# Row numbers of the first expert tile from a comparison with the ranks of expert 0, and one summed set for the routing table and the gates

## The chip, the core and the metric

One Trainium2 chip, of which the kernel uses one core. The metric is device time in microseconds (us) of one execution, start to end. The kernel before takes 900.72 us (median of 3 runs, 900.62 to 901.5).

## What is computed

One step of a one-layer decoder trunk over 1056 tokens (a prompt of 1024 and 8 samples of 4), each a row of 1024 float32 numbers:

```python
x <- LN1(alpha * x + Mixer(x))      # one input projection, conv / pool / gated conv, one output projection
x <- LN2(alpha * x + HierMoE(x))

def hier_moe(xt):                                    # xt: 1056 x 1024
    g_logits = xt @ w_rg + b_rg                      # 4 expert groups, top 1
    e_logits = xt @ w_re + b_re                      # 4 experts in the chosen group, top 2
    top_w = softmax(top_v) * g_p
    for e in range(16):                              # SwiGLU, 1024 -> 512 -> 1024
        h = silu(xt @ w_gate[e]) * (xt @ w_up[e])
        y = y + gate[:, e:e + 1] * (h @ w_down[e])
```

## The kernel before, in words

The program is written engine by engine, with semaphores between the engines; each engine works through its own list in order. There are three parts: the mixer, the routing, and the expert tiles. A short last part adds up and normalises.

**Expert tiles.** Tokens are sorted by expert into tiles of 128 rows, each tile of one expert (here 26 tiles for 16 experts). Per tile, POOL fetches the rows from DRAM (`x1_rows`) by an indirect DMA (L670), PE turns them (8 transposes, L1293), ACT rounds them into a high part (L938 for the first tile) and DVE makes the low part (L1229); with high and low parts of rows and weights PE multiplies three times for each product (L1564 gate and up, in two halves of 24 matmuls each; L1580 down). The weights of an expert come in six units of 1 MB: units 0 to 3 hold gate and up, units 4 and 5 hold down. ACT makes each unit's high part, DVE the low part (`lo_unit`, L328). A tile's first half (`h == 0`) takes six matmuls from unit 0, six from unit 1 and so on, and waits for each unit's low part. After 18 matmuls of the second half PE turns the first half of the hidden values, which DVE has multiplied (L1243). SP reloads a unit for the next expert when its low part is made.

**Routing.** When all logits are there, DVE chooses for each token a group and two experts (L1134 to L1156: `Mb` is 1 where a token chose an expert). PE sums over the choices (L1510 to L1517): the rank of a token within each expert, and how many tokens each expert has. From the counts DVE makes the first and the last tile of each expert (L1161 to L1167), from ranks and first tiles each choice's place: its tile `tcol` and its row in the tile `rlf` (L1172 to L1183). Then come one-hot sets: `ohe`, which tile (L1187, 630 elements a partition), `oht`, the same times the token number and times a correction (L1189, L1191), and `ohp`, which row (L1194, two of 1152 elements). PE multiplies `ohp` by `oht` (L1524): the sum in PSUM is the table of row numbers for every tile. Meanwhile DVE makes the gates of the choices (L1199 to L1204), then takes the table out of PSUM (L1206, L1207). Only then POOL copies the first tile's column into `idxc` (L665), does a one-element add behind which the copy is sure to be written (L669), and sends the indirect DMA of the first rows (L670). While they travel, DVE splits the gates into three bfloat16 parts (L1211 to L1214), multiplies them into `ohe` (`otw`, three ops, L1216), PE sums these too (L1546, 105 columns), and DVE makes the low parts of units 1 and 2 (L328). After the first tile's rows are split, DVE adds up the gate parts (L1233 to L1235) and makes the low parts of units 3, 4 and 5.

POOL asks for the second tile's rows after the first rows have landed and PE has turned them: copy L665, add L669, DMA L670.

## Time and profile before

| | |
|---|---|
| median of 3 runs | 900.72 us |
| the profiled execution | 900.35 us |
| its span (first to last instruction) | 898.7 us |
| PE busy, DVE busy, ACT busy, POOL busy | 91%, 65%, 49%, 30% of the span |
| mean granted TensorE clock | 0.956 of full speed |
| logits complete, start of routing on DVE | 362.1 us |
| first indirect DMA sent | 381.4 us |
| PE starts the first expert tile | 389.4 us |

The profile lists instructions with start, duration and what released them, all in us from the start of the span. PE is the matmul engine, DVE the vector engine, ACT the scalar engine, POOL the general one, SP issues DMAs. A line such as L328 is a line of the kernel; a line in a helper stands for all its callers. The clock of PE is granted at one of two levels, 1.2 and 2.4 GHz, shown as 0.5 and 1.0.

### The profile page before, as it was taken

The numbers are of one execution on the slowest core, as the hardware profiler recorded it, in microseconds if no ns is written. First come the engines' busy times: TensorE is split into PE (matmuls) and PEld (weight loads), VectorE is DVE, ScalarE is ACT, GpSimd is POOL, SyncE is SP. The second block draws the span as 40 slices with busy tenths as digits, with TensorE's granted clock in tenths as the row PEclk, the third lists the DMA queues.
The fourth block names the chain that finished last, engine by engine and source line by source line (L and its number), as shares of the span: only waits on it lengthen the run. The fifth ranks groups of instructions, "written<-read, shape, count | busy, mean of one in ns | idle before, by whom it ended". The sixth has DMA issues, their size and how long they took to land.

```text
span 898.7 us, 12722 instructions
## 1 busy us (share of the span) xinstructions
PE 822.1 (91%) x4275; PEld 715.2 (80%) x4276; DVE 587.9 (65%) x732; ACT 442.2 (49%) x494; POOL 268.8 (30%) x259
## 2 busy tenths in 40 slices
PE   6999999999999999289999999999999999999900
PEld 6999999998788886168888888888888888888800
DVE  4099999957666555889889982158821614837148
ACT  5311132546633224338888883359733725846233
POOL 1423564562000000024433441224321313323225
PEclk9999999999999999579999999999999999999955
DMA  8211111103656331479999998149952663973164
GB/s 289 55 48 47 47 47 47 47 1 114 241 196 251 117 121 47 153 245 320 392 384 379 394 393 289 28 132 375 374 190 59 213 174 93 363 263 88 24 237 172
DMA packets 59407, 167.34 MB, mean 186 GB/s; under 512 B 6757, under 2 KB 25190, under 8 KB 55286
## 3 DMA queue, kind: packets, MB, share of 16 engines
q1 hardware_dynamic: 51318, 144.57, 43.0%
q0 software_dynamic: 8064, 22.45, 11.6%
q8 instruction: 14, 0.23, 0.1%
q14 instruction: 11, 0.09, 0.0%
HBM read 144.79 MB, written 28.24 MB: 193 GB/s over the span
## 4 chain that ended last, share of the span: by engine, by line
PE 89%; DVE 6%; DMA 2%; ACT 1%; issue 1%; POOL 0%; SPq 0%; POOLq 0%; ACTq 0%; DVEq 0%
PE PS L1564 32%; PE PS L1315 19%; PE PS L1580 16%; PE PS L1494 10%; PE PS L1293 6%; DVE C L1073 1%; PE PS L1342 1%; PE PS L1465 1%; PE PS L1382 1%; DVE RAW L1270 1%; PE PS L1446 1%; DVE BIG L387 1%; DMA sum_rows<-F,MIX 1%; DMA F<-in_x_prompt 1%; DMA F<-x_rows,MIX 0%
## 5 line engine op out<-in xcount | busy, mean ns | idle before, releaser
L1564 PE MATMUL PS<-BIG,TH 128*128 128x512 f32 x1248 | 296.3, 394 | 1.5 <-DVE TH L1229 1.5
L1564 PEld LDWEIGHTS PS<-BIG,TH 128*128 128x128 f32 x1248 | 233.9, 189 | 49.5 <-issue 1.9
L1315 PE MATMUL PS<-BIG,WD 128*128 128x352 f32 x1080 | 177.3, 325 | 0.0
L1315 PEld LDWEIGHTS PS<-BIG,WD 128*128 128x128 f32 x1080 | 174.9, 188 | 0.9
L328 DVE TENSOR_TENSOR BIG<-RAW,BIG 128x2048 fp32r<-128x2048 f32 x64 | 145.1, 2288 | 24.3 <-ACT BIG L901 24.3
L1580 PE MATMUL PS<-WD,TH 128*128 128x512 f32 x624 | 155.8, 399 | 0.0
L1580 PEld LDWEIGHTS PS<-WD,TH 128*128 128x128 f32 x624 | 113.5, 189 | 21.9
L901 ACT ACTIVATE BIG<-RAW 128x2048 fp32r<-128x2048 f32 x64 | 119.2, 1908 | 15.5 <-PE PS L1494 7.9
L292 DVE SCALAR_TENSOR_TENSOR PS<-RAW,C,PS 128x512 f32<-128x512 f32 x174 | 115.4, 752 | 0.0
L1494 PE MATMUL PS<-BIG,WD 128*128 128x512 f32 (+1 forms) x432 | 100.7, 392 | 1.8 <-DVE BIG L387 1.8
L1494 PEld LDWEIGHTS PS<-BIG,WD 128*128 128x128 f32 (+1 forms) x432 | 76.7, 179 | 22.7 <-issue 1.3
L669 POOL TENSOR_TENSOR MIX<-C 128x1 f32<-128x1 f32 x28 | 33.5, 1198 | 189.2 <-PE PS L1293 189.0
L1243 DVE TENSOR_TENSOR F<-F,PS 128x256 f32<-128x256 f32 x52 | 21.8, 420 | 93.4 <-ACT F L944 81.1
L328 DVE TENSOR_TENSOR WD<-MIX,WD 128x2048 fp32r<-128x2048 f32 x32 | 72.0, 2289 | 9.6 <-ACT WD L901 9.6
L1293 PEld LDWEIGHTS PS<-C,F 128*128 128x128 f32 (+1 forms) x408 | 60.9, 188 | 13.9 <-issue 6.3
L1293 PE MATMUL PS<-C,F 128*128 128x128 f32 (+1 forms) x408 | 62.8, 284 | 7.5 <-DMA F<-in_x_prompt 6.7
L550 POOL TENSOR_TENSOR WD<-F,WD 128x1024 fp32r<-128x1024 f32 x17 | 41.0, 2409 | 76.5 <-ACT WD L718 76.3
L901 ACT ACTIVATE WD<-MIX 128x2048 fp32r<-128x2048 f32 x32 | 59.6, 1907 | 3.3 <-DMA MIX<-in_w_down 3.3
L1247 DVE TENSOR_TENSOR TH<-PS,TH 128x256 fp32r<-128x256 f32 x52 | 21.9, 421 | 56.4 <-ACT TH L950 33.4
L965 ACT ACTIVATE F<-PS,MIX 128x1024 f32<-128x1024 f32 x26 | 29.1, 1119 | 49.4 <-PE PS L1580 49.4
L692 POOL TENSOR_TENSOR MIX<-C 128x1 f32<-128x1 f32 x26 | 18.9, 728 | 108.1 <-ACT F L965 108.1
L693 POOL DMA_INDIRECT sum_rows<-F,MIX x26 | 41.9, 1610 | 7.8 <-issue 7.8
(203 smaller groups left out, 762.6 us busy)
## 6 DMA issues: line engine op xcount, KB each, us to landing
RAW<-in_w_gate SPq DMA_DIRECT2D x64, 512.0 KB, 7.1
RAW<-in_w_up SPq DMA_DIRECT2D x64, 512.0 KB, 9.3
MIX<-in_w_down SPq DMA_DIRECT2D x32, 1024.0 KB, 10.4
F<-in_w_in SPq DMA_DIRECT2D x17, 512.0 KB, 4.1
F<-in_x_prompt SPq DMA_DIRECT2D x10, 512.0 KB, 4.7
x_rows<-F SPq DMA_DIRECT2D x9, 512.0 KB, 2.6
sum_rows<-F SPq DMA_DIRECT2D x9, 512.0 KB, 3.6
RAW<-in_w_out SPq DMA_DIRECT2D x4, 1024.0 KB, 6.2
```

Of the source, the lines that this page charges most:

```text
L292: ins = eng.scalar_tensor_tensor(accs[h] if j < TAPS - 1 else outs[h], ins_[h], w, accs[h], ALU.mult, ALU.add)
L328: eng.tensor_tensor(by_row(u, l), raw_rows(u), by_row(u, unit_parts(u)[0].bitcast(F32)), ALU.subtract).then_inc(S("unit_lo"), 1)
L550: pool.tensor_tensor(win[:, q, 1], wraw[q].rearrange("p (k m) -> p k m", k=KD), win[:, q, 0].bitcast(F32), ALU.subtract).then_inc(S("win_l ...
L669: pool.tensor_tensor(carrier[:, 0:1], epsc, epsc, ALU.add)
L693: pool.indirect_dma_start(acc_dram, bass.IndirectOffsetOnAxis(ap=scat, axis=0), yrow, None, compute_op=ALU.add).then_inc(S("y_stored"), 16)
L901: act.activation(by_row(u, h), raw_rows(u), ACT.Copy).then_inc(S("unit_hi"), 1)
L965: act.activation(yrow, PS[:, 5:7, :].rearrange("p b n -> p (b n)"), ACT.Copy, scale=gates[:, ds(t, 1)]).then_inc(S("y_copied"), 1)
L1293: return pe.transpose(out, in_, ident[0:n, 0:n])
L1315: mm = pe.matmul(bank(3 * q + g, GRP), win[:, q, ws, c, :], xT[:, xs_, c, g * GRP:(g + 1) * GRP], start=(c == 0 and ws + xs_ == 0), stop=( ...
L1494: mm = pe.matmul(bank(out_bank(i, h), rows=M), mhl[:, i % 2, ms, c, 0:M], wo[:, ws, c, h * 512:(h + 1) * 512], start=(c == 0 and ms + ws = ...
L1564: mm = pe.matmul(bank(h), xe[:, xs_, c, :], w, start=(c == 0 and xs_ + ws == 0), stop=(c == KD - 1 and xs_ == 1))
L1580: mm = pe.matmul(bank(5 + h), he[:, hs, c, :], wd[:, ws, c, h * 512:(h + 1) * 512], start=(c == 0 and hs + ws == 0), stop=(c == KF - 1 and ...
```

## The change

For the first tile alone the row numbers are made without the table. A token that chose expert 0 sits in the first tile in the row of its rank within expert 0, so one comparison of `igf` (row numbers less 1024) with `key0` (rank less 1024 where the token chose expert 0) gives the one-hot set `ohf` (1152 elements a partition, bfloat16). PE multiplies it by `vc0`, two columns: the token numbers and a correction (9 matmuls, into bank 5); DVE adds these to `idxc` directly, and POOL sends the first indirect DMA from that, with no copy and no add of its own.

The table is made afterwards, and together with the gates: `otw` now has five sets of columns (token number, correction, three gate parts) and PE sums 175 columns in one set of 18 matmuls, which stands behind the 8 transposes of the first rows. DVE makes the first two of the five; the three products with the gate parts move from DVE to POOL. The gates' values are made ahead of the ranks. The low parts of units 1 and 2 move from before the split of the first rows to behind the table.

```diff
@@ gpsimd
+                gather_rows()
+
+            def gather_rows():
                 pool.indirect_dma_start(xg, None, x1_dram, bass.IndirectOffsetOnAxis(ap=idxc, axis=0),
...
+            pool.wait_ge(S("x1_stored"), 16 * NT)
+            pool.wait_ge(S("first_index"), 1)
+            gather_rows()
+            pool.wait_ge(S("columns_hot"), 1)
+            for h in range(3):
+                pool.tensor_tensor(otw[:, :, :, 2 + h, :], ohe,
+                                   part[h].rearrange("p k (i m) -> p k i m", m=1).to_broadcast((P, 2, NT, NTAB)),
+                                   ALU.mult).then_inc(S("gate_hot"), 1)
+            pool.wait_ge(S("rows_in"), 16)
             pool.wait_ge(S("table_ready"), 1)
-            index(0)
-            pool.wait_ge(S("x1_stored"), 16 * NT)
-            gather(0)
-            pool.wait_ge(S("rows_in"), 16)
             index(1)
             pool.wait_ge(S("xe_turned"), 1)
             gather(1)
@@ vector
+            dve.tensor_copy(vc0[:, :, 0], tokid[:, 0:NT]).then_inc(S("first_values"), 1)
...
+            dve.wait_ge(S("exps"), 2)
+            do(dve.tensor_reduce(gsum, ge, AX, ALU.add))
...
+            do(dve.tensor_tensor(wgt[:, 1], wgt[:, 0], ex, ALU.mult))
             dve.wait_ge(S("ranked"), 1)
+            do(dve.scalar_tensor_tensor(key0, Mb[:, :, 0], -float(FAR), rk[:, :, 0], ALU.mult, ALU.add))
+            dve.tensor_scalar(vc0[:, :, 1], key0, -1.0, pm, ALU.mult, ALU.add).then_inc(S("first_values"), 1)
+            dve.wait_ge(S("x1_ready"), NT)
+            dve.tensor_tensor(ohf, igf.rearrange("p (i m) -> p i m", i=1).to_broadcast((P, NT, P)),
+                              key0.rearrange("p (i m) -> p i m", m=1).to_broadcast((P, NT, P)), ALU.is_equal
+                              ).then_inc(S("first_hot"), 1)
             counts_ps = bank(7)[:, NT * NE:(NT + 1) * NE]
...
+            dve.wait_ge(S("first_sum"), 1)
+            do(dve.tensor_copy(firstf, bank(5, 2)))
+            dve.scalar_tensor_tensor(idxc, firstf[:, 0:1], padc, firstf[:, 1:2], ALU.add, ALU.add
+                                     ).then_inc(S("first_index"), 1)
+            do(dve.tensor_copy(part[0], wgt))
...
-            do(dve.tensor_tensor(ohe, it.rearrange("p (k i m) -> p k i m", k=1, i=1).to_broadcast(four),
-                                 tcol.rearrange("p k (i m) -> p k i m", m=1).to_broadcast(four), ALU.is_equal))
-            do(dve.tensor_tensor(oht[:, :, :, 0, :], ohe, tokid[:, 0:NT].rearrange("p (k i m) -> p k i m", k=1, m=1
+            dve.tensor_tensor(ohe, it.rearrange("p (k i m) -> p k i m", k=1, i=1).to_broadcast(four),
+                              tcol.rearrange("p k (i m) -> p k i m", m=1).to_broadcast(four), ALU.is_equal
+                              ).then_inc(S("columns_hot"), 1)
+            dve.wait_ge(S("columns_hot"), 1)
+            do(dve.tensor_tensor(otw[:, :, :, 0, :], ohe, tokid[:, 0:NT].rearrange("p (k i m) -> p k i m", k=1, m=1
...
-            for h in range(3):
-                dve.tensor_tensor(otw[:, :, :, h, :], ohe,
...
-            lo_unit(dve, 0, 1)
-            lo_unit(dve, 0, 2)
...
             ins.then_inc(S("xe_lo"), 1)
-            dve.wait_ge(S("gate_sum"), 1)
-            do(dve.tensor_copy(gatep, bank(7, 3 * NTAB)))
...
+            dve.wait_ge(S("table_sum"), 1)
+            do(dve.tensor_copy(tabf, bank(6, 5 * NTAB)))
+            dve.scalar_tensor_tensor(table, tabf[:, 0:NTAB], padc, tabf[:, NTAB:2 * NTAB], ALU.add, ALU.add
+                                     ).then_inc(S("table_ready"), 1)
+            for u in (1, 2, 3):
+                lo_unit(dve, 0, u)
...
-            for u in (3, 4, 5):
+            for u in (4, 5):
                 lo_unit(dve, 0, u)
@@ tensor
+            pe.wait_ge(S("first_values"), 2)
+            pe.wait_ge(S("first_hot"), 1)
+            for i in range(NT):
+                M = rows_of(i)
+                mm = pe.matmul(bank(5, 2), ohf[0:M, i], vc0[0:M, i], start=(i == 0), stop=(i == NT - 1))
+            mm.then_inc(S("first_sum"), 1)
...
             mm.then_inc(S("xe_turned"), 1)
+            pe.wait_ge(S("gate_hot"), 3)
+            for c in range(2):
+                pe.wait_ge(S("one_hot"), c + 1)
+                for i in range(NT):
+                    M = rows_of(i)
+                    mm = pe.matmul(bank(6, 5 * NTAB), ohp[0:M, c, i], otw[0:M, c, i].rearrange("p h m -> p (h m)"),
+                                   start=(c + i == 0), stop=(c == 1 and i == NT - 1))
+            mm.then_inc(S("table_sum"), 1)
```

How the lists of the engines change, at two places. First DVE, from the one-hot sets to the last unit of expert 0. Before:

```order
L1187 TENSOR_TENSOR RAW<-MIX 128x630 [waits x1_ready,route_steps]
L1189 TENSOR_TENSOR RAW<-RAW,MIX 128x18x35 [waits route_steps]
L1191 TENSOR_TENSOR RAW<-RAW,MIX 128x18x35 [waits route_steps]
L1194 TENSOR_TENSOR RAW<-MIX 128x1152 [waits route_steps]
...
L1216 TENSOR_TENSOR MIX<-RAW,MIX 128x18x35 [waits route_steps]
L1216 TENSOR_TENSOR MIX<-RAW,MIX 128x18x35 x2
L328 TENSOR_TENSOR BIG<-RAW,BIG 128x2048 [waits unit_hi] x2
L1229 TENSOR_TENSOR TH<-PS,TH 128x512 [waits half_hi]
L1229 TENSOR_TENSOR TH<-PS,TH 128x512 [waits xe_hi]
L1233 COPY MIX<-PS 128x105 [waits gate_sum]
```

and now (L331 is the old L328, L1241 the old L1229):

```order
L1221 TENSOR_TENSOR RAW<-MIX 128x630 [waits route_steps]
L1225 TENSOR_TENSOR MIX<-RAW,MIX 128x18x35 [waits columns_hot]
L1227 TENSOR_TENSOR MIX<-RAW,MIX 128x18x35 [waits route_steps]
L1230 TENSOR_TENSOR RAW<-MIX 128x1152 [waits route_steps]
L1230 TENSOR_TENSOR RAW<-MIX 128x1152
L1241 TENSOR_TENSOR TH<-PS,TH 128x512 [waits half_hi]
L1241 TENSOR_TENSOR TH<-PS,TH 128x512 [waits xe_hi]
L1245 COPY MIX<-PS 128x175 [waits table_sum]
L1246 SCALAR_TENSOR_TENSOR MIX<-MIX 128x35 [waits route_steps]
L331 TENSOR_TENSOR BIG<-RAW,BIG 128x2048 [waits unit_hi] x3
```

The three products of 18x35 are gone from DVE, and the two units that stood ahead of the split of the rows stand behind the table. Second POOL, around the first two fetches. Before:

```order
L665 COPY MIX<-MIX 128x1 [waits table_ready]
L669 TENSOR_TENSOR MIX<-C 128x1 [waits index_copied,x1_stored]
L670 DMA F<-x_rows,MIX 128x1024
L665 COPY MIX<-MIX 128x1 [waits rows_in]
L669 TENSOR_TENSOR MIX<-C 128x1 [waits index_copied,xe_turned]
L670 DMA F<-x_rows,MIX 128x1024
```

and now:

```order
L676 DMA F<-x_rows,MIX 128x1024 [waits first_index,x1_stored]
L685 TENSOR_TENSOR MIX<-RAW,MIX 128x18x35 [waits columns_hot]
L685 TENSOR_TENSOR MIX<-RAW,MIX 128x18x35 x2
L668 COPY MIX<-MIX 128x1 [waits table_ready,rows_in]
L672 TENSOR_TENSOR MIX<-C 128x1 [waits index_copied,xe_turned]
L676 DMA F<-x_rows,MIX 128x1024
```

The first DMA stands ahead of the table's work and the three products stand between it and the second fetch, which now waits for the table.

## Rows read from the trace of the kernel before

**Rows 1.** The page, part 4: the chain that ended last, shares by engine.
```profile
PE 89%; DVE 6%; DMA 2%; ACT 1%; issue 1%; POOL 0%; SPq 0%; POOLq 0%; ACTq 0%; DVEq 0%
```

**Rows 2.** Busy time by stretch: us, each engine busy (instructions), PEclk, DMA share, GB/s.
```profile
380.00:390.00 10.00, 4.70 (x28) 3.63 (x29) 9.56 (x16) 1.49 (x3) 4.72 (x6) 0.50 0.37 117
390.00:400.00 10.00, 10.00 (x38) 8.09 (x37) 6.90 (x4) 2.80 (x3) 1.62 (x1) 0.82 0.97 326
```

**Rows 3.** The chain that ended last, in order of time: start us, us, what.
```profile
381.41 4.45 DMA F<-x_rows,MIX
...
385.91 1.99 PE PS L1293 x8
...
389.38 11.80 PE PS L1564 x42
...
409.43 9.53 PE PS L1564 x42
```

**Rows 4.** Timeline of DVE, routing to first tile: start us, us, line, op, [idle before].
```profile
369.22 0.17 DVE L1161 TENSOR_SCALAR MIX<-PS 128x16 int32<-128x16 f32 x1 [1.12 <-PE PS L1517]
...
370.44 0.30 DVE L1172 SCALAR_TENSOR_TENSOR MIX<-MIX,PS 128x144 f32<-128x144 f32 x1
...
373.25 0.82 DVE L1187 TENSOR_TENSOR RAW<-MIX 128x630 f32<-128x630 f32 x1 [0.20 <-DVE MIX L1183]
...
375.80 2.63 DVE L1194 TENSOR_TENSOR RAW<-MIX 128x1152 bf16<-128x1152 f32 x2
...
379.47 0.17 DVE L1204 TENSOR_TENSOR MIX<-MIX 128x9 f32<-128x9 f32 x1
...
379.94 0.26 DVE L1207 SCALAR_TENSOR_TENSOR MIX<-MIX 128x35 uint32<-128x35 f32 x1
...
380.74 0.18 DVE L1214 TENSOR_TENSOR MIX<-MIX 128x18 bf16<-128x18 f32 x1
380.96 2.26 DVE L1216 TENSOR_TENSOR MIX<-RAW,MIX 128x630 bf16<-128x630 f32 x3
383.14 4.49 DVE L328 TENSOR_TENSOR BIG<-RAW,BIG 128x2048 fp32r<-128x2048 f32 x2
387.69 0.69 DVE L1229 TENSOR_TENSOR TH<-PS,TH 128x512 fp32r<-128x512 f32 x1
...
389.15 0.26 DVE L1233 COPY MIX<-PS 128x105 f32<-128x105 f32 x1
...
397.54 0.42 DVE L1243 TENSOR_TENSOR F<-F,PS 128x256 f32<-128x256 f32 x1 [1.06 <-ACT F L944]
```

**Rows 5.** Timeline of PE: the sums of the gates.
```profile
383.28 2.11 PE L1546 MATMUL PS<-MIX,RAW 128*128 128x105 bf16 x18 [3.98 <-DVE MIX L1216]
```

**Rows 6.** Timeline of POOL: around the second tile's fetch.
```profile
385.92 1.75 POOL L665 COPY MIX<-MIX 128x1 uint32<-128x1 uint32 x1 [3.16 <-DMA F<-x_rows,MIX]
...
388.68 1.06 POOL L670 DMA_INDIRECT F<-x_rows,MIX  x1 [0.52 <-issue]
394.90 1.62 POOL L665 COPY MIX<-MIX 128x1 uint32<-128x1 uint32 x1 [5.17 <-DMA F<-x_rows,MIX]
```

**Rows 7.** Timeline of POOL and DVE in the mixer, 46 to 50 us.
```profile
46.42 2.39 POOL L550 TENSOR_TENSOR WD<-F,WD 128x1024 fp32r<-128x1024 f32 x1
46.48 2.68 DVE L277 TENSOR_TENSOR MIX<-RAW,C 128x248 f32<-128x248 f32 x1 [18.36 <-POOL RAW L560]
49.08 0.90 DVE L277 TENSOR_TENSOR MIX<-RAW,C 128x248 f32<-128x248 f32 x2
```

**Rows 8.** POOL's groups by shape: count, busy us, mean ns, idle before.
```profile
L590 POOL TENSOR_TENSOR MIX<-RAW 128x1038 f32<-128x1038 f32 x2 | 3.8, 1914 | 0.0
L591 POOL TENSOR_TENSOR RAW<-RAW 128x144 f32<-128x144 f32 x2 | 0.8, 422 | 0.0
```

**Rows 9.** DMA issues, 380 to 560 us: median us from issue to landing.
```profile
F<-x_rows,MIX POOLq DMA_INDIRECT x11, 7.0
```

**Rows 10.** Waits, 380 to 860 us: who for whom, us in total, times, longest.
```profile
ACT WD L901 <- DMA MIX<-in_w_down: 0.8, 1, 0.8
```

More of the change, by code:

```diff
@@ L207, in build @@
         wrem = [mx(2 * NT).rearrange("p (k i) -> p k i", k=2) for _ in range(2)]
+        part = [wpart[0][:, 0], wpart[0][:, 1], wpart[1][:, 0]]
         ohp = RAW[:, OFF_BC:OFF_BC + NT * P].bitcast(BF16).rearrange("p (k i m) -> p k i m", k=2, i=NT)
-        oht = RAW[:, OFF_BC + NT * P:OFF_BC + NT * (P + 2 * NTAB)].bitcast(BF16
-                  ).rearrange("p (k i h m) -> p k i h m", k=2, i=NT, h=2)
-        ohe = RAW[:, OFF_BC + NT * (P + 2 * NTAB):OFF_BC + NT * (P + 4 * NTAB)
-                  ].rearrange("p (k i m) -> p k i m", k=2, i=NT)
-        tabf = mx(2 * NTAB)
+        ohe = RAW[:, OFF_BC + NT * P:OFF_BC + NT * (P + 2 * NTAB)].rearrange("p (k i m) -> p k i m", k=2, i=NT)
+        ohf = (RAW[:, OFF_BC + NT * (P + 2 * NTAB):OFF_BC + NT * (P + 2 * NTAB) + NT * P // 2].bitcast(BF16)
+               .rearrange("p (i m) -> p i m", i=NT))
+        igf, key0, pm = mx(P), mx(NT), mx(1)
+        vc0 = mx(NT).bitcast(BF16).rearrange("p (i w) -> p i w", w=2)
+        firstf = mx(2)
+        tabf = mx(5 * NTAB)
         table = mx(NTAB).bitcast(U32)
         idxc = mx(1).bitcast(U32)
-        otw = mx(3 * NT * NTAB).bitcast(BF16).rearrange("p (k i h m) -> p k i h m", k=2, i=NT, h=3)
-        gatep = mx(3 * NTAB)
+        otw = mx(5 * NT * NTAB).bitcast(BF16).rearrange("p (k i h m) -> p k i h m", k=2, i=NT, h=5)
         gates = mx(NTAB)
@@ L1519, in _ @@
             mm.then_inc(S("ranked"), 1)
-            for c in range(2):
-                pe.wait_ge(S("one_hot"), c + 1)
-                for i in range(NT):
-                    M = rows_of(i)
-                    mm = pe.matmul(bank(6, 2 * NTAB), ohp[0:M, c, i], oht[0:M, c, i].rearrange("p h m -> p (h m)"),
-                                   start=(c + i == 0), stop=(c == 1 and i == NT - 1))
-            mm.then_inc(S("table_sum"), 1)
+            pe.wait_ge(S("first_values"), 2)
[4 more added lines that the diff above has]
+            mm.then_inc(S("first_sum"), 1)
             def turn_xe(t):
@@ L1538, in turn_hid @@
                 mm.then_inc(S("hid_turned"), 1)
-            for c in range(2):
-                for i in range(NT):
-                    M = rows_of(i)
-                    if c + i == 0:
-                        pe.wait_ge(S("gate_hot"), 3)
-                    mm = pe.matmul(bank(7, 3 * NTAB), ohp[0:M, c, i], otw[0:M, c, i].rearrange("p h m -> p (h m)"),
-                                   start=(c + i == 0), stop=(c == 1 and i == NT - 1))
-            mm.then_inc(S("gate_sum"), 1)
             pe.wait_ge(S("rows_in"), 16)
```

41 lines of the change are left out of this document (15 added, 26 removed).

## The prediction, made before the changed kernel ran

> **What bounds the kernel now.** I read the page's chain first: PE holds 89% of it, DVE 6%, DMA 2% [rows 1]. PE cannot be helped by this change except where it waits, so I then read the busy time by stretch: from 380 to 390 us PE is busy 4.70 of 10 us and DVE 9.56 [rows 2]. That is the routing. The chain in order of time says what PE waits for there: the indirect DMA of the first rows, sent at 381.41 and landed 4.45 us later, 8 transposes, the split, and the first tile at 389.38 [rows 3]. After that the chain is PE alone to the last tile, so a first tile that ends earlier by x should end the kernel earlier by x, unless something else is late. The last view, DVE's timeline, tells what else: DVE has hardly a pause from the choices to unit 5. While the rows travel it makes three products (2.26 us) and the low parts of units 1 and 2 (4.49), and its split of the rows starts 0.06 us after those [rows 4]. The rows' travel is thus already full of DVE work; an earlier landing finds DVE in arrears. So the question is how far DVE's own list is shortened, and whether POOL's help is free.
>
> **How POOL and DVE get on.** POOL's 2.39 us operation of 46.42 ends at 48.81; a DVE product of two SBUF inputs that starts at 46.48 takes 2.68 us, to 49.16, while the next two take 0.90 together [rows 7]. It stood still until POOL had ended. The other way round, POOL's one-element copies at 385.92 and 394.90 take 1.75 and 1.62 us, and the first ends at 387.67, when the second of DVE's L328 has ended (383.14 + 4.49 = 387.63) [rows 4, 6]. I read this as: a DVE instruction with two SBUF inputs and a POOL instruction exclude each other for their whole length, and the waiting one goes at the next boundary. [...]
>
> **The sum, on the clock of the profile.** Each step by its rows.
> - Up to the choices: one added copy of 9 elements, 0.1 us. The choices are made at 368.10 (DVE idles 1.12 before 369.22) [rows 4].
> - The gates' six small operations move here: from the end of L1194 at 378.43 to the end of L1204 at 379.64 they took 1.2 us [rows 4]. The 1.12 us wait for the ranks covers them but for 0.1 to 0.2. At 369.5 `key0` and the correction follow, two at 0.2, then `ohf`, 1152 elements like each half of L1194 (2.63 / 2 = 1.31) [rows 4]: 371.2.
> - PE's 9 matmuls of two columns take at most half of the gates' 18 (2.11 / 2 = 1.05) [rows 5], and lie beside the counts, which took 369.22 to 370.44 = 1.22 [rows 4]: 372.4. Two small operations give `idxc`, 0.4 to 0.5 (L1207 is 0.26) [rows 4]: 372.9.
> - POOL sends the DMA at 373 to 374.1 (before, 1.21 us lay between L1207's end at 380.20 and the DMA at 381.41, copy and add included); with 4.45 us [rows 3] the rows land at 377.5 to 378.6, 7 to 8 us earlier than before. The transposes, 1.99 [rows 3], end by 380.6. None of that is on the path, as follows.
> - DVE goes on: four splits of the gates, 0.72 (380.20 to 380.92), then ranks to places, 370.44 to 373.25 = 2.81, `ohe` 0.82 [rows 4]: 377.2. Before, `ohe` ended at 374.07; this is the 3.1 us that the short cut costs.
> - From 377.2 DVE has two products and two one-hot sets, which took 374.10 to 378.43 = 4.33 [rows 4], and POOL its three products of 630 elements. POOL's price is not in the trace for this shape. From below: the step from 144 to 1038 elements is 1.49 us [rows 8], so 0.42 + 486 x 1.67 ns = 1.23. From nearby above: 2.39 x 630 / 1024 = 1.47 [rows 7]. I take 1.45, since L550 like these writes another type than it reads. A bfloat16 input on POOL is not shown; the outer end is the 2.39 of the full 1024. All of it excludes DVE's: 4.33 + 3 x 1.45 = 8.7, DVE free at 385.9, whichever begins; POOL done at about 384.6.
> - The Trainium skill, GPSIMD Engine Reference, When to use GPSIMD, says to keep two-input elementwise work on VectorE, GpSimd being about twice as slow; by that the three would cost 4.5 instead of 2.26 us, and the sum would be later by 0.2 than mine.
> - PE: 18 matmuls of 175 columns, by columns 2.11 x 175 / 105 = 3.5 [rows 5]; nine from 384.6, nine once the last one-hot set is there at 385.9: 387.9. Meanwhile DVE splits the rows, two at 0.69 [rows 4], to 387.3.
> - First tile: PE starts at about 388.0 instead of 389.38. DVE takes 175 columns (105 took 0.26; 0.35) and makes the table (0.26) [rows 4]: 388.5, then units 1, 2, 3 at 4.49 / 2 = 2.25 each: 390.8, 393.0, 395.3.  Six matmuls cost 6 x 9.53 / 42 = 1.36 at the full clock and up to twice that, 2.7, at the low one (the first tile's 42 took 11.80; the granted clock is 0.50 from 380 to 390, 0.82 from 390 to 400) [rows 2, 3]. So PE now waits for units 1, 2 and 3, and its first half ends at 395.3 + 1.36 = 396.7; before, 18 matmuls (4.1) ahead of 389.38 + 11.80 = 401.18, that was 397.1.
> - Gain 0.4 us. Next late is DVE: gates 0.4, units 4 and 5 4.49, first hidden product 0.42: 400.6, needed at 396.7 + 4.1 = 400.8 (before it was there at 397.96, three us ahead) [rows 4]. If this cover of 0.2 us goes, each further delay of DVE costs the same on PE.
>
> The later loads of expert 1 (units 1 to 5 are loaded when their low parts are made, now 3 to 5 us later) I cost at nothing: from 380 to 860 us ACT waited for weights once, 0.8 us [rows 10]. The three DVE products and POOL's copy and add for the first tile are removed at no gain of their own; they are in the sum.
>
> **Forecast:** 0.4 us less. The profiled execution of 900.35 becomes 899.95; the median of the runs is 0.37 above it, so 900.3. A measurement of this kernel tells 0.2%, 1.8 us, from no change. The bounds of POOL's price move DVE's list by 3 x (1.23 - 1.45) = -0.7 to 3 x (2.39 - 1.45) = +2.8.
>
> **Rivals.**
> 1. *POOL and DVE run side by side.* Then DVE and POOL are both done at 381.6, PE's table at 385.2, DVE's table at 385.8, unit 3 at 392.6, the first half at 393.9: 3.2 us less, with the hidden product (397.9) just in time. An earlier PE meets the weights where ACT already waited 0.8 us [rows 10], which may take up to as much back. 897.5 to 898.3. For it: the rows show full exclusion at two shapes only, neither with a bfloat16 result. [...] Against: [rows 6, 7]. Chance 0.16.
> 2. *The second fetch comes late (slower).* It now needs the table and then three turns of POOL against DVE's units: copy at 390.8, add at 393.0, DMA at about 393.6, which if shut out until 395.3 lands 7.0 us later [rows 9] at 402.3. PE wants these rows when its second half ends, 396.7 + 24 x 0.227 = 402.2. Before, they landed at 394.9 (389.74 + 5.17) [rows 6], six us ahead. It decides from 402.2 on: one turn missed (2.25 us, and once shut out behind unit 4, 2.2 more than in the sum) makes 404.5 to 404.7, PE waits 2.4, net +2.0 to +2.5: 902.7 to 903.2. Against: both copies in rows 6 got in at the first boundary they met. Chance 0.11.
> 3. *The clock stays low while PE waits for units.* Then six matmuls take up to 2.7 us, more than DVE's 2.25 a unit, the first half ends by 390.8 + 8.1 = 398.9, up to 1.8 later than before: up to 902.5. Against: the clock rose between 390 and 400 (0.82, so at about 393.6) behind PE work that began at 389.38 [rows 2, 3]; now PE works from 384.6. Chance 0.06.
> 4. *POOL's products are dear* (bfloat16 input, 2.39 each): +2.8 - 0.4 = +2.4, 903.1. Chance 0.07.
>
> The forecast has 0.60. Faster by over 1.8 us: rival 1, 0.16. Slower by over 1.8: rivals 2 and 4, 0.18. Within: 0.66. The range leaves out about 0.2: most of rival 1 and rival 4 with the far end of rival 2: 898.2 to 902.8; the forecast's own, with POOL between 1.23 and 1.6 and the second fetch up to 1 us late, is 899.6 to 901.7.
>
> **What would show it.** In the changed profile: the first indirect DMA at 373 to 374; POOL's three products (L685) and DVE's L1225 to L1230 stretched, each about as long as the other's turn, and ending at 385 to 386; PE's table at 388; L1579 with waits for L331; the first tile ending within 1 us of 409.4. Products of POOL of 1.5 us beside DVE's of normal length, or a first tile that ends before 408, would make it wrong; so would PE waiting for rows of the second tile at 402.

## The result, and the profile after the change

The changed kernel takes 902.66 us (median of 15 runs, 900.14 to 904.35), the kernel before 900.83 in the same comparison (15 runs): ratio 1.0016, 95% interval 1.0009 to 1.0023, or 1.4 us more (the two medians lie 1.8 apart). The forecast was 0.4 us less. The time lies in the range, and the change is below the 0.2% that the prediction took as the least to be told from no change; but it is clear of the noise here, and on the other side. Run twice more (below), the same kernel gave 0.9997 and 1.0004, neither clear of no change: its executions spread from 899.8 to 904.4, and in one of the three comparisons they fall in two separate groups, near 900.3 and near 903. What parts those that were profiled is shown below.

The profiled execution took 903.01 us, its span is 901.1. Where the time went is plainest from PE's start of each tile (the first L1579 of the tile in PE's timeline; L1564 before), in us; the last two columns are a repetition of the changed kernel and of its difference from before:

| tile | before | after | difference | after, repeated | difference |
|---|---|---|---|---|---|
| 0 | 389.38 | 386.56 | -2.82 | 386.88 | -2.50 |
| 1 | 409.27 | 407.14 | -2.13 | 407.58 | -1.69 |
| 7 | 516.09 | 513.84 | -2.25 | 514.38 | -1.71 |
| 8 | 533.91 | 535.58 | +1.67 | 533.93 | +0.02 |
| 25 | 836.23 | 838.03 | +1.80 | 836.37 | +0.14 |

The first tile gains much more than the 0.4 us forecast, and keeps it for seven tiles. Then one tile, that of expert 7, takes 21.74 us instead of 17.82, and from there on every tile is later than before. All other tiles from 1 on take 17.8 in both kernels. Behind the start of the last tile lie 63.0 us in the profile after, 62.5 before and 62.6 in the repeated one.

**At the front.** The timelines of DVE and POOL after the change (start us, us, line, op, idle before), to be read against [rows 4, 6]:

```profile
375.95 0.82 DVE L1221 TENSOR_TENSOR RAW<-MIX 128x630 f32<-128x630 f32 x1
376.80 0.82 DVE L1225 TENSOR_TENSOR MIX<-RAW,MIX 128x630 bf16<-128x630 f32 x1
377.65 1.74 DVE L1227 TENSOR_TENSOR MIX<-RAW,MIX 128x630 bf16<-128x630 f32 x1
379.43 4.59 DVE L1230 TENSOR_TENSOR RAW<-MIX 128x1152 bf16<-128x1152 f32 x2
383.94 1.27 DVE L1241 TENSOR_TENSOR TH<-PS,TH 128x512 fp32r<-128x512 f32 x2
386.04 0.34 DVE L1245 COPY MIX<-PS 128x175 f32<-128x175 f32 x1 [0.83 <-PE PS L1567]
386.42 0.26 DVE L1246 SCALAR_TENSOR_TENSOR MIX<-MIX 128x35 uint32<-128x35 f32 x1
386.59 6.69 DVE L331 TENSOR_TENSOR BIG<-RAW,BIG 128x2048 fp32r<-128x2048 f32 x3
```
```profile
373.48 1.12 POOL L676 DMA_INDIRECT F<-x_rows,MIX  x1 [10.58 <-DVE MIX L1198]
376.86 5.94 POOL L685 TENSOR_TENSOR MIX<-RAW,MIX 128x630 bf16<-128x630 f32 x3 [2.26 <-DVE RAW L1221]
386.83 2.09 POOL L668 COPY MIX<-MIX 128x1 uint32<-128x1 uint32 x1 [4.03 <-DVE MIX L1246]
389.06 2.06 POOL L672 TENSOR_TENSOR MIX<-C 128x1 f32<-128x1 f32 x1
391.30 2.94 POOL L676 DMA_INDIRECT F<-x_rows,MIX  x1 [0.17 <-issue]
400.36 0.40 POOL L668 COPY MIX<-MIX 128x1 uint32<-128x1 uint32 x1 [6.12 <-DMA F<-x_rows,MIX]
```

The two engines take turns. DVE's second product, alike in size to the first, takes 1.74 instead of 0.82, and the two one-hot sets 4.59 instead of 2.63 [rows 4], while POOL's three products take 5.94. PE in the same stretch, and the stretches as a whole (us, then each engine's busy time and instructions, the granted clock of PE, DMA share, GB/s; the DMA share is the mean busy share of the core's 16 DMA engines):

```profile
382.86 3.15 PE L1567 MATMUL PS<-MIX,RAW 128*128 128x175 bf16 x18 [3.12 <-POOL MIX L685]
386.56 4.31 PE L1579 MATMUL PS<-BIG,TH 128*128 128x512 f32 x12 [0.55 <-issue]
391.13 1.65 PE L1579 MATMUL PS<-BIG,TH 128*128 128x512 f32 x6 [0.26 <-DVE BIG L331]
393.33 5.74 PE L1579 MATMUL PS<-BIG,TH 128*128 128x512 f32 x24 [0.55 <-DVE BIG L331]
```
```profile
380.00:390.00 10.00, 6.59 (x27) 4.94 (x28) 9.14 (x8) 1.65 (x2) 5.83 (x4) 0.53 0.03 5
390.00:400.00 10.00, 9.19 (x40) 7.01 (x39) 9.90 (x8) 3.92 (x3) 4.07 (x2) 1.00 0.94 328
```

Against [rows 2], PE is busy 6.59 us of the ten from 380 on instead of 4.70, and its clock is at the upper level (1.00) through the next ten. But the DMA engines carry 5 GB/s from 380 to 390, where they carried 117. The loads of expert 1's weights wait for the low parts that DVE now makes behind the table. SP's timeline of the kernel before and then of the changed one, the loads of units 1, 2 and 4:

```profile
385.45 0.33 SPq L372 DMA_DIRECT2D RAW<-in_w_gate  x1
...
387.65 0.33 SPq L372 DMA_DIRECT2D RAW<-in_w_gate  x1
...
394.31 2.53 SPq L377 DMA_DIRECT2D MIX<-in_w_down  x2
```
```profile
388.90 0.33 SPq L375 DMA_DIRECT2D RAW<-in_w_gate  x1
...
391.11 0.33 SPq L375 DMA_DIRECT2D RAW<-in_w_gate  x1
...
395.84 2.53 SPq L380 DMA_DIRECT2D MIX<-in_w_down  x2
```

Units 1 and 2 start 3.45 us later, unit 3 1.2 and units 4 and 5 1.5 us later, while PE, which is going to use them, is 2 to 3 us earlier. From expert 2 on the loads go out 2.1 us earlier than before (unit 0 at 400.88 instead of 402.99), since they follow PE.

**At the tile of expert 7.** ACT's and PE's timelines after the change:

```profile
521.16 1.91 ACT L912 ACTIVATE BIG<-RAW 128x2048 fp32r<-128x2048 f32 x1
525.38 1.91 ACT L912 ACTIVATE BIG<-RAW 128x2048 fp32r<-128x2048 f32 x1 [2.31 <-DMA RAW<-in_w_up]
527.20 0.36 ACT L961 ACTIVATE TH<-PS 128x256 fp32r<-128x256 f32 x1
```
```profile
524.99 1.05 PE L1309 MATMUL PS<-C,F 128*128 128x128 f32 x8
528.15 1.93 PE L1595 MATMUL PS<-WD,TH 128*128 128x512 f32 x6 [2.11 <-DVE TH L1263]
...
530.16 5.58 PE L1595 MATMUL PS<-WD,TH 128*128 128x512 f32 x18
```

ACT stands 2.31 us before the high part of expert 8's unit 1, because half of that unit has not landed. Behind it in ACT's list stands L961, the high part of the hidden values (L950 before), then DVE's L1263, and PE waits for that, 2.11 us. The chain that ended last goes back through the same load ("511.04 14.26 DMA RAW<-in_w_up"): the load took 14.26 us from its issue. Behind its wait PE's matmuls are stretched, 18 of them to 5.58 us.

In the kernel before ACT made the high parts of units 0 and 1 in one go here:

```profile
523.17 3.94 ACT L901 ACTIVATE BIG<-RAW 128x2048 fp32r<-128x2048 f32 x2 [0.23 <-PE PS L1564]
```

The two take 1.91 each, so that of unit 1 began at about 525.2, behind a pause of 0.1 us. The same half unit landed at 525.12 there, and at 525.30 in the changed kernel: it came just in time before, and it comes no earlier now. The changed kernel asks for it 2.0 us earlier, at the end of unit 0's high part (523.07), and waits.

In the repeated profile of the changed kernel the rows of PE read:

```profile
528.08 1.65 PE L1595 MATMUL PS<-WD,TH 128*128 128x512 f32 x6 [1.49 <-DVE TH L1263]
...
529.72 4.38 PE L1595 MATMUL PS<-WD,TH 128*128 128x512 f32 x18
```

There the wait is 1.49, and 18 matmuls take 4.38. The granted clock tells the two apart: from 530 to 535 us it is 0.73 in the first profile and 1.00 in the second. So the loss is a load that comes later than ACT wants it, and in some executions a fall of PE's clock behind the wait on top of it. In the first comparison the mean granted clock of an execution fits that: 0.958 or 0.959 in the seven fastest (900.14 to 902.62 us), 0.954 to 0.957 in the eight slowest (902.66 to 904.35). In the two others the clocks of fast and slow executions overlap, and the seven without a fall are themselves 2.5 us apart, so the fall is not all that parts them. The tile takes 19.55 us in the repeated profile, 1.7 over the 17.82 before; in the first it is 3.9 over, 0.6 of the difference from a longer wait and 1.6 from the slower matmuls (1.93 - 1.65, 5.58 - 4.38, and two transposes between them).

Why is that load late? Busy time by stretch, the kernel before and then the changed one:

```profile
395.00:415.00 20.00, 20.00 (x96) 16.71 (x95) 15.44 (x12) 15.05 (x13) 8.68 (x7) 1.00 0.87 305
415.00:520.00 105.00, 105.00 (x498) 87.82 (x497) 94.39 (x66) 92.94 (x78) 43.35 (x35) 1.00 1.02 382
...
560.00:600.00 40.00, 40.00 (x194) 33.59 (x193) 9.24 (x14) 14.80 (x19) 7.28 (x13) 1.00 0.22 41
```
```profile
395.00:415.00 20.00, 20.00 (x95) 16.76 (x95) 19.03 (x14) 16.94 (x15) 5.84 (x7) 1.00 1.01 382
415.00:520.00 105.00, 105.00 (x499) 87.93 (x498) 94.44 (x67) 92.79 (x77) 43.41 (x36) 1.00 1.03 387
```

The first eight experts have one tile each, so each of their tiles brings six new units of weights. From 415 us on the DMA engines are busy all the time in both kernels (share 1.0, 382 to 387 GB/s), and the loads fall behind: the time from issue to landing grows over the stretch. For units 4 and 5 of expert 1, and of expert 8 (DMA issues of 388.5 to 399 us and of 519 to 523, KB each, median us to landing):

```profile
MIX<-in_w_down SPq DMA_DIRECT2D x2, 1024.0 KB, 8.0
```
```profile
MIX<-in_w_down SPq DMA_DIRECT2D x2, 1024.0 KB, 14.8
```

Expert 8 has four tiles, so that fewer loads are wanted, and from 560 to 600 us the share is 0.22. The tile of expert 7 is thus the last of the stretch, where the backlog is largest, and unit 1 is what ACT asks for early in a tile. In the kernel before the same tile had no such wait, PE being 2.2 us later.

### The profile page after: what moved, and what is told of

Read it like the earlier page. It is cut to its first block, busy times and chain, and to the rows that moved or that the text cites. A ratio compares the mean times of both kernels' runs of the same rounds, so it can differ in the third digit from the quotient of the medians.

```text
span 901.1 us, 12711 instructions
## 1 busy us (share of the span) xinstructions
PE 823.7 (91%) x4266; PEld 715.8 (79%) x4267; DVE 590.3 (66%) x734; ACT 441.6 (49%) x494; POOL 273.2 (30%) x262
## 4 chain that ended last, share of the span: by engine, by line
PE 87%; DVE 7%; DMA 3%; issue 1%; ACT 1%; POOL 1%; SPq 0%; ACTq 0%; POOLq 0%; DVEq 0%
PE PS L1579 30%; PE PS L1331 19%; PE PS L1595 15%; PE PS L1510 10%; PE PS L1309 6%; PE PS L1481 2%; DMA RAW<-in_w_up 2%; DVE C L1084 1%; PE PS L1358 1%; PE PS L1398 1%; DVE BIG L331 1%; DVE RAW L1286 1%; PE PS L1462 1%; DMA sum_rows<-F,MIX 1%; DVE BIG L390 1%
## 5 line engine op out<-in xcount | busy, mean ns | idle before, releaser
L1579 PE MATMUL PS<-BIG,TH 128*128 128x512 f32 x1248 | 296.2, 393 | 1.4 <-DVE BIG L331 0.8
L1579 PEld LDWEIGHTS PS<-BIG,TH 128*128 128x128 f32 x1248 | 233.3, 189 | 49.7 <-DVE BIG L331 1.8
L331 DVE TENSOR_TENSOR BIG<-RAW,BIG 128x2048 fp32r<-128x2048 f32 x64 | 145.0, 2289 | 21.9 <-ACT BIG L912 21.8
L331 DVE TENSOR_TENSOR WD<-MIX,WD 128x2048 fp32r<-128x2048 f32 x32 | 72.0, 2288 | 10.3 <-ACT WD L912 10.2
L1263 DVE TENSOR_TENSOR TH<-PS,TH 128x256 fp32r<-128x256 f32 x52 | 21.9, 422 | 59.5 <-ACT TH L961 36.2
```

Of the source, the lines that this page charges most:

```text
L331: eng.tensor_tensor(by_row(u, l), raw_rows(u), by_row(u, unit_parts(u)[0].bitcast(F32)), ALU.subtract).then_inc(S("unit_lo"), 1)
L1579: mm = pe.matmul(bank(h), xe[:, xs_, c, :], w, start=(c == 0 and xs_ + ws == 0), stop=(c == KD - 1 and xs_ == 1))
```

## The experiments

Theory (A): the DMA engines are the bound from 389 to 530 us; the lead of PE and the late start of the loads (A1) add up to what is lost in the tile of expert 7, and with less to carry, or an earlier start, the front's gain stays. By A2 the late start costs nothing. Rivals: the loss is one of ACT's order, of PE's clock, or of the one chip; or only PE's lead counts. Each comparison has its own runs of the kernel before beside it (medians 900.78 to 901.21).

**Less to load.** For experts 3 to 5 only the first half of unit 5 is loaded, 1.6 MB less in all.

```diff
-                sp.dma_start(unit_raw(u), src).then_inc(S(f"unit_raw{u}"), 16)
+                sp.dma_start(unit_raw(u)[:, 0:rows, :], src[:, 0:rows, :]).then_inc(S(f"unit_raw{u}"), 16)
...
+            with sp.Fori(3, 6) as e:
+                load_expert(e, 1)
```

In the changed kernel:

> The changed kernel, but unit 5 of experts 3, 4 and 5 is loaded by half (0.5 MB less each; the other half is stale, so these experts' down products are not the reference's). Theory A: the changed kernel's first tile ends 2.1 us earlier and PE keeps that for seven tiles; it loses it in the tile of expert 7, where ACT waits 2.3 us for weights of expert 8 because the loads have fallen behind. With 1.5 MB less ahead of it, some 4 us of loading at 390 GB/s, that wait is gone: no wait of ACT for a load near 525 us, the clock stays at 1.0 there, and the time is the one before less about 2.2: 898.6 us. Theory B: the loss there has another cause (code, order of the engines) and does not hang on the volume loaded: 902.7 us as the changed kernel.

In the kernel before:

> The kernel before with the same half loads of unit 5 of experts 3, 4 and 5. It is the control. Theory A: there the loads are just in time (ACT waits once, 0.8 us, and PE not at all), so less to load gives nothing: 900.8 us, within 0.3. If the cut itself sped up the program, this one would fall as well, to 899 or less, and after_cut would prove nothing.

Measured 898.83 us, ratio 0.9974 (0.9961 to 0.9986), and 900.29, ratio 0.9992 (0.9978 to 1.0005). In the first the tile of expert 7 takes 17.8, ACT waits for no load, and unit 1's landing takes 10.8 us instead of 14.3. The late load is the loss, and without it the change is worth 1.5 us against this control, 2 against the kernel before.

**Less to scatter.** Tiles are filled up to 128 rows; the rows behind an expert's last token were added into a row that nobody reads. Here they are left out.

```diff
-                                        compute_op=ALU.add).then_inc(S("y_stored"), 16)
+                                        bounds_check=TOK - 1, oob_is_err=False, compute_op=ALU.add).then_inc(S("y_stored"), 16)
```

In the changed kernel:

> The changed kernel, except that the scatter leaves out the rows behind an expert's last token (their row number is beyond the table), which otherwise are added to a row that nobody reads: 26 x 128 - 2112 = 1216 rows of 4 KB, some 5 MB of writes and as much reading for the addition. What is computed stays the same. Theory A (the DMA engines are busy all the time from 395 us on and fall behind the loads by some us until expert 8; less traffic brings the loads forward): the last part of unit 1 of expert 8 lands 2 us earlier or more, ACT's wait of 2.3 us in the tile of expert 7 goes, and the time is 898.6. Rival B (rows of the scatter cost the engines that carry the loads nothing, or the loads are bound by something else than the engines): the wait stays at 2 us and the time is that of the changed kernel, 900.9 to 902.7.

In the kernel before:

> The kernel before with the same scatter that leaves the rows behind an expert's last token out. Control: there PE stands 2.8 us later at tile 0, and ACT's wait for expert 8's unit 1 was 0.2 us, so theory A expects no change, 900.6 to 900.9. If less traffic is worth time for a reason of its own, this one is faster too, and what after_skip gains more than this one is what the wait had cost.

Measured 898.93 us, ratio 0.9969 (0.9957 to 0.9981), and 900.64, ratio 0.9992 (0.9978 to 1.0005). The rows of the late load, from the DMA issues of 510.5 to 513.5 us, in the changed kernel and then with the leaner scatter:

```profile
RAW<-in_w_up SPq DMA_DIRECT2D x1, 512.0 KB, 14.3
```
```profile
RAW<-in_w_up SPq DMA_DIRECT2D x1, 512.0 KB, 9.9
```

Against its control the change is worth 1.7 us here. Rows of POOL's scatter thus cost the engines that SP's loads use. The DMA share alone would not have told these kernels from the changed one: from 415 to 520 us it is 1.02 with the shorter loads (371 GB/s) and 0.99 with the leaner scatter (369 GB/s), and both keep PE's lead. The Trainium skill, DMA: Bandwidth & Descriptors, "Issuing engines are not separate DMA queues", says that DMAs of all engines run on the same 16 DMA engines and interleave; these two runs agree.

**The changed kernel again**, beside these and beside a later set.

> The changed kernel once more, nothing edited, as the measure for the three kernels beside it. Theory A (the 2.8 us that tile 0 gains are given back in the tile of expert 7, where ACT waits 2.3 us for the last part of expert 8's unit 1 and PE 2.1 us for ACT, with a clock that falls behind that wait in some executions and not in others): 900.9 to 902.7, the tile of expert 7 takes 20.2 us without a fall of the clock and 21.8 with one, against 17.8 in the tiles beside it. Rival B (the loss seen was one chip's, not the kernel's): 898.6, all tiles alike.

> The changed kernel once more, as the measure for the three beside it: 900.2 to 902.7, with executions in two groups, near 900.3 where the clock holds in the tile of expert 7 and near 903 where it falls behind PE's wait.

Measured 900.75 (0.9997, 0.9983 to 1.0011): eight executions from 899.81 to 901.07 and four from 902.49 to 903.69. Then 901.88 (1.0004, 0.9989 to 1.0018), 900.92 to 902.85; its profile shows the wait of 2.1 us with the 18 matmuls at 5.66.

**ACT's order.** The load that is late stands ahead of the hidden values in ACT's list; here it stands behind them.

```diff
-                    for u in (0, 1):
-                        act.wait_ge(S("unit_used"), 6 * t + u + 1)
-                        hi_unit(e + 1, u)
+                    act.wait_ge(S("unit_used"), 6 * t + 1)
+                    hi_unit(e + 1, 0)
...
+                if last:
+                    act.wait_ge(S("unit_used"), 6 * t + 2)
+                    hi_unit(e + 1, 1)
```

> The changed kernel, except that ACT makes the high part of the next expert's unit 1 behind the high part of the hidden layer's first half instead of ahead of it, in every expert's tile. Theory A (PE's 2.1 us in the tile of expert 7 are ACT's queue: the load that is late stands there ahead of the hidden values that PE wants, and PE doesn't want unit 1 itself before the next tile): PE no longer waits for the hidden values, the tile of expert 7 takes 17.8 us, and the lead of tile 0 stays, unless the late load is missed at the start of the next tile: 898.6 to 899.5. Rival B (PE is bound by the load itself, whatever the order of ACT): the same 2 us are lost at the start of the tile of expert 8, and the time is 900.9 or above.

Measured 907.6 us, ratio 1.0064 (1.0047 to 1.0081). ACT no longer waits for a load, but each such tile takes 18.4 us instead of 17.8: unit 1's low part comes later on DVE and stands ahead of the second half of the hidden values there. That wait of PE is about half of the 0.6 us. The row of PE's waits (us in total, times, longest) is from 386 to 860 us:

```profile
PE PS L1597 <- DVE TH L1265: 4.8, 15, 0.3
```

Both theories missed; the order that loses once in the tile of expert 7 saves 0.6 us in the tiles of other experts.

**PE kept busy while it would wait.** Sixteen matmuls of 256 columns more, in the tile of expert 7 (`"busy"` marks that expert's tile).

```diff
+                for _ in range(16 if last == "busy" else 0):
+                    pe.matmul(bank(7, 2 * P), TRI[:, 1, :], TRI[:, :, :].rearrange("p s m -> p (s m)"), start=True, stop=True)
...
-            expert_tiles(pe, tile)
+            expert_tiles(pe, tile, 7)
```

> The changed kernel, with 16 matmuls of 256 columns without use, into a free bank, in the tile of expert 7 alone, between the transposes of the next rows and the wait for the low part of the hidden values, where PE stood for 2.1 us. Theory A: the wait itself stays (the weights come when they come), but the clock, which fell to 0.5 from 529 to 533 us behind that wait, stays at 1.0, which gives back about 1.8 us: 900.9 us. If the fall of the clock costs nothing beside the wait: 902.7 us. If the matmuls only delay: up to 904.

Measured 901.53 (1.0001, 0.9988 to 1.0014), 900.25 to 902.38.

```profile
526.39 1.91 PE L1597 MATMUL PS<-TRI 128*128 128x256 bf16 x16
529.13 1.70 PE L1604 MATMUL PS<-WD,TH 128*128 128x512 f32 x6 [0.84 <-DVE TH L1270]
...
530.82 4.37 PE L1604 MATMUL PS<-WD,TH 128*128 128x512 f32 x18
```

1.91 us of work and 0.84 of wait: PE starts the next step at the same distance behind the load as before, and none of the 12 executions is above 902.38, where the upper group of the repeated comparison began at 902.49. The wait was time in which PE could do other work. That the clock never falls so is likely by these numbers, not shown beyond them, since a profile of the next experiment has the full wait and no fall either.

**The products back on DVE.** The three gate products of L685 are made by DVE.

```diff
-            pool.wait_ge(S("columns_hot"), 1)
-            for h in range(3):
-                pool.tensor_tensor(otw[:, :, :, 2 + h, :], ohe,
...
+            for h in range(3):
+                dve.tensor_tensor(otw[:, :, :, 2 + h, :], ohe,
```

> The changed kernel with the three products of the gate parts back on DVE, behind its own two and ahead of the one-hot sets; POOL does none. If POOL and DVE exclude each other (forecast): DVE is free at about 383.3 instead of 384.0, its products take 0.82 and 0.75, the one-hot sets 1.31 each again, the table's sum is ready about 1.0 us earlier (385 instead of 386) and the first tile ends about 1.0 earlier (406.1). The total then hangs on the loads (theory A): the gain is lost in the tile of expert 7, 902 to 903 us. If POOL's products had run beside DVE's for free: DVE's list is longer by 2.3 us and the first tile ends 2 us later, 409; the total is 901 to 905.

Measured 900.59 (0.9992, 0.9977 to 1.0006).

```profile
376.67 0.81 DVE L1216 TENSOR_TENSOR RAW<-MIX 128x630 f32<-128x630 f32 x1
377.51 0.82 DVE L1220 TENSOR_TENSOR MIX<-RAW,MIX 128x630 bf16<-128x630 f32 x1
378.37 0.82 DVE L1222 TENSOR_TENSOR MIX<-RAW,MIX 128x630 bf16<-128x630 f32 x1
379.22 2.26 DVE L1225 TENSOR_TENSOR MIX<-RAW,MIX 128x630 bf16<-128x630 f32 x3
381.40 2.62 DVE L1229 TENSOR_TENSOR RAW<-MIX 128x1152 bf16<-128x1152 f32 x2
```

With POOL still, every DVE operation has its own length again, and from the start of the mask `ohe` to the last one-hot set it is 7.35 us (376.67 to 384.02) instead of 8.06 (375.95 to 384.01). Handing three products to POOL cost 0.7 us net. The tile of expert 7 still loses time, PE's wait there being 2.1.

**PE late, or loads late.** The changed kernel starts PE earlier and the loads later. First the 16 added matmuls in the tile of expert 2, which takes the lead away (`expert_tiles(pe, tile, 2)` in the diff above):

> The changed kernel, except that PE makes 16 matmuls of 256 columns more in the tile of expert 2 (into a bank that nobody reads, 1.9 us), so that PE's lead over the kernel before falls from 2.2 us to 0.3 before the tile of expert 7. Theory A (the lead can't be kept past the late load of expert 8 in any case): the wait in the tile of expert 7 shrinks to 0.3 us or nothing, that tile takes 17.8 to 18.1 us, and the time is that of the changed kernel without the clock's fall, 900.5, with none of its executions above 902; the 1.9 us of work cost nothing. Rival B (the lead is worth its time to the end, and the loss in tile 7 is one of its own): 1.9 us on top of the changed kernel, 902.6 or above.

Measured 900.45 (0.9994, 0.9985 to 1.0002), eleven of the twelve executions between 899.82 and 901.75. By the time, 1.9 us of added work cost nothing, as theory A had it. The profile, which is of the slowest execution (903.09), does not bear it out: there PE waits 2.57 us in the tile of expert 7, its lead over the kernel before being 0.48. The load itself landed at 527.5 there, 2.2 us later than in the changed kernel, about as much as PE had been held up. So a small lead alone does not save an execution from the late load, and the landing is not fixed in time whatever PE does. A landing is told in 16 parts; 15 of this one were in at 523.87, and the last came 3.7 us behind them. Why is open.

Then the loads of expert 1 a step later, in both kernels, PE's own order unchanged:

```diff
-            load_expert(1)
+            for u in range(6):
+                wait_lo(sp, 0, min(u + 1, 5) if u else 0)
+                load_unit(sp, 1, u)
```

In the changed kernel:

> The changed kernel, except that SP issues the loads of expert 1's units 1 to 4 one step of expert 0's low parts later (each 2.2 us; unit 5 as it was). PE's work and its order are the same. Theory A1 (the DMA engines, without a break from 389 to 530 us, carry what the late start of expert 1's loads leaves behind through to the last load of the stretch): ACT's wait in the tile of expert 7 grows from 2.3 to 4.5 us, that tile takes 22 us or more, and the time is 902.9 to 904.5. Theory A2 (only PE's earlier start matters; a late start of the loads is made up on the way): the wait stays at 2.3 us, 900.5 to 902.5.

In the kernel before:

> The kernel before with the same loads of expert 1 a step later (units 1 to 4, by 2.2 to 4.4 us), so that they start as late as in the changed kernel while PE starts tile 0 as late as before. Theory A1 (start of the loads): ACT's wait in the tile of expert 7 is 2.4 us in place of 0.2, the tile takes 20 to 22 us, and the time is 903. Theory A2 (only PE's lead): no wait, 900.8.

Measured 903.53 (1.0023, 1.0009 to 1.0036) and 902.28 (1.0015, 1.0001 to 1.0030; before beside it 900.99). PE's timelines of the changed kernel in the tiles of experts 5 and 7, then of the kernel before in that of expert 7:

```profile
493.59 1.65 PE L1597 MATMUL PS<-WD,TH 128*128 128x512 f32 x6 [2.68 <-DVE TH L1265]
...
530.05 1.65 PE L1597 MATMUL PS<-WD,TH 128*128 128x512 f32 x6 [0.60 <-DVE TH L1265]
```
```profile
529.61 1.65 PE L1582 MATMUL PS<-WD,TH 128*128 128x512 f32 x6 [2.62 <-DVE TH L1249]
```

With units 1 to 4 of expert 1 2.2 to 2.5 us later than in the repeated profile of the changed kernel, PE waits 2.68 + 0.60 = 3.3 us, two tiles sooner in part, where it waited 1.49 to 2.11. Tile 0 starts at the same time in these two profiles (386.83 and 386.88), no clock falls, and tile 8 starts at 535.89 instead of 533.93, 2.0 us later. The time alone says less: 903.53 lies 0.9 above the first comparison of the changed kernel and 2.8 above the second. The kernel before, which lost nothing, now has the wait of the changed one and nearly its time. Not all of that wait is the loads' doing: in this profile tile 1 starts at 408.02, 1.25 us earlier than in the one of [rows 3], 0.7 of it from an earlier tile 0. But tile 8 starts at 535.45, 1.5 us later than before. So later loads cost time in both kernels, in the changed one most of their delay (A1); A2 explains neither profile. In the changed kernel itself no such cost is seen at that load, which landed as it did before.

Last the opposite: DVE makes one low part in the gap before the table, and so the loads start earlier.

```diff
+            lo_unit(dve, 0, 1)
             dve.wait_ge(S("table_sum"), 1)
...
-            for u in (1, 2, 3):
+            for u in (2, 3):
                 lo_unit(dve, 0, u)
```

> The changed kernel, except that DVE makes the low part of expert 0's unit 1 before the table is taken over (at 385.2 us, where it waits 0.8 us for PE's sum) in place of behind it, so that the first of expert 1's loads starts 1.4 us earlier, at 387.5, and the second tile's row numbers 1.5 us later, rows at 401.9 (PE wants them at 403). Theory A1: ACT's wait in the tile of expert 7 falls from 2.3 to 0.9 us and the time to 899.3 to 900. Theory A2: the wait stays, 900.5 to 902.5, or is more by as much as PE starts earlier.

> The same unit ahead of the table, with the three gate products on DVE in place of POOL (the table's columns are ready 0.7 us earlier, and so are the loads that follow). Theory A1: PE and loads both start 0.7 us earlier than in the kernel with the gap filled alone, the wait stays near 0.9 us, and the time is 898.6 to 899.3. Theory A2: the wait is 2.3 us or more, 900.5 or above.

Measured 899.67 (0.9987, 0.9973 to 1.0002): eight executions from 898.69 to 899.97, four from 902.08 to 902.55. Both groups lie about 1 us below those of the second comparison of the changed kernel, but the interval takes in no change. The profile fell in the upper group and has the wait still (2.0 us), so the smaller wait that A1 expected is not seen there; only the time agrees. With the products on DVE as well: 900.11 (0.9992, 0.9976 to 1.0009), 897.93 to 903.86, profile with a wait of 1.1 us, another of 0.4 us for the second tile's rows, and a span of 897.4; too spread to say more.

**Both repairs.** The products on DVE, with the leaner scatter, and with the shorter loads:

> The changed kernel with the three gate products on DVE, the engine that makes the table's columns, in place of POOL, and with the scatter that leaves the rows behind an expert's last token out. Theory A (POOL and DVE run such operations one at a time, so the products on DVE cost less than on POOL, and with less traffic no load is late): tile 0 starts 0.7 us earlier after the mask of expert 0 than in the changed kernel, the tile of expert 7 takes 17.8 us, and the time is 0.5 to 0.7 less than with the leaner scatter alone, 898.3. Rival B (2.8 us of lead are as much as the loads allow even so): the time is 898.9, with a wait of ACT for a load somewhere.

> The changed kernel with the three gate products on DVE in place of POOL, and with only one half of the last unit loaded for experts 3 to 5 (their second half is what an earlier expert left there, so that the output of these experts is another; 1.6 MB less to load). Theory A: 0.5 to 0.7 less than with the shorter loads alone (898.8), 898.2, and no wait of ACT for a load. Rival B (the products on DVE are worth nothing at this place): 898.8.

Measured 898.22 (0.9964, 0.9951 to 0.9976; 897.01 to 898.55) and 897.96 (0.9969, 0.9958 to 0.9980). No wait for a load in either profile, and they are 0.7 and 0.9 us below the kernels with POOL's products and the same scatter or loads, as expected, though by less than the intervals tell. The first computes all that the kernel before computes and is faster than both kernels: 0.9964 of the kernel before.

## Why the prediction was right and wrong

- *The exclusion of POOL and DVE* was right, and so rival 1 (side by side) was wrong: the two take turns, one whole instruction each, with a bfloat16 result too, which the prediction had no row for. The Trainium skill, GPSIMD Engine Reference, Specifications, gives contention with DVE instructions that have two SBUF inputs, which these have; the trace agrees (1.74 us for 0.82). That should have lowered the rival's 0.16.
- *POOL's price*, 1.45 us each, was mis-sized. DVE's four operations took 7.24 us (376.77 to 384.01) instead of their own 4.33, so POOL's three cost 2.91, or 0.97 each, below even the lower bound of 1.23. With `ohe` 0.4 us earlier (0.2 of it by an earlier start of the routing), DVE was free at 384.01 instead of 385.9 and the table's sum done at 386.0 instead of 387.9. That the sum is over 2.0 us behind DVE's last set was right, though half of the 3.5 us that the prediction gives the 18 matmuls would be 1.8.
- *PE waits for units 1, 2 and 3* was right in kind: two waits for L331, 0.26 and 0.55 us. With the clock up from 389.4 on, rival 3 did not come; in the repeated profile, where it rose at 392.9, PE waited for no unit and tile 0 took 0.1 us more. The first half's last unit was ready at 393.3 instead of 395.3.
- *The second fetch* (rival 2): POOL's copy and add did wait for DVE's boundaries, 2.09 and 2.06 us, as worked out; the rows were there at 400.4, PE did not wait.
- So the gain at the first tile was sized at 0.4 and was 2.1 by tile 1 (1.7 in the repeated profile), about 1.9 without the earlier start of the routing. Most of the difference is POOL's price, 3 x (1.45 - 0.97) = 1.4 us.
- **The step that failed** is "The later loads of expert 1 ... I cost at nothing", and with it "a first tile that ends earlier by x should end the kernel earlier by x". The ground given was that ACT had waited for weights once, 0.8 us [rows 10]. But the absence of waits showed that the loads arrived in time with PE where it was, not that they had time to spare. What the runs showed in its place: expert 8's unit 1 had no time to spare before (ACT already paused 0.1 us for it) and landed no earlier after, so that PE's lead of 2.2 us (1.7 in the repeated profile) became ACT's wait of 2.3 (1.9). The tile of expert 7 grew by 1.7 us, and by 3.9 where the clock fell behind the wait; with less traffic the loss is gone. The growing landing times that would have told it were not read. That the time lies in the stated range all the same is luck: a gain 1.7 us larger than forecast met a loss that the sum did not have. Rivals 2 and 4 name times near 902.7 too, by mechanisms that did not come (PE did not wait for rows, and POOL was cheaper).
- Rival 1's remark that an earlier PE "meets the weights" named the mechanism, and bounded it by that 0.8 us. The bound is the lead itself: what PE gained went, and when the loads were made later still, most of that was lost on top. How the loss of the changed kernel divides between PE's lead and the later start of expert 1's loads is not settled, since no run moves PE alone without moving the loads that follow it.
- Of the signs to look for, one was named that would prove the sum wrong, a first tile that ends before 408, and it came: 407.14. None looked beyond tile 1, where the time was decided.

## What to carry to other kernels

Before a gain at the front is booked at the end, ask of every later stretch how long before its use each load lands. That nobody waits for a load does not say that it has time to spare: here the decisive one had none, and an earlier consumer only made the wait. Landing times that grow from load to load are the sign to look for; a DMA share near 1.0 marks the stretch, but it is 1.0 as well in the kernels that kept the gain. A reordering that delays what frees load buffers delays the loads behind it, so price the issue times of the queue as well as the engines. Here 1.5 to 2 us of the front's gain showed at the end only when traffic was taken out of that stretch.

## What the runs showed of the hardware that was not expected

- POOL's product of 630 elements to bfloat16 costs DVE 0.97 us, while the 1038-element one took 1.91 and the 144-element one 0.42 [rows 8]; by those it would be 1.23.
- PE's clock after a wait of about two microseconds fell in some profiles and not in others: it fell behind waits of 2.02, 2.09 and 2.11 us (0.73 from 530 to 535 us in the last), and not behind one of 2.12 with the products on DVE, nor behind 2.57, 2.62 and 2.68. What decides it is not settled.
- Two profiles of the changed kernel have waits of 1.49 and 2.11 us for the same load, and its landing took 13.7 and 14.3 us; with most of the lead taken away (16 matmuls in the tile of expert 2) it took 14.7. What makes it differ from one execution to the next is open too. But the trace shows where to look: a load's landing is told in 16 parts, and a few of them come late. Of this load half were in 10.2 us from the issue in the first profile, the 15th after 12.4 and the last after 14.3; with the lead taken away it was 9.5, 11.0 and 14.7. The DMA share is a mean over the 16 engines and does not show such a straggler.
